# Modulation chunks in pairs over one bank, placed in norms and attention; scores ahead of older transposes; low parts on one engine

## The reference, cut to what matters

```python
# two hybrid layers (l = 0, 1), each:
shift, scale, gate = split(silu(c) @ w_mod[l] + b_mod[l], 3)          # 1024 -> 3 x 1024, also for c_ctx
h = rms_norm(x, norm_w) * (1 + scale) + shift
p = h @ w_in ;  y = [MLA attention 6 heads, GQA attention 6 heads, conv] * silu(gate columns of p)
x = x + gate * (y @ w_out)
# then a second block of two layers (i = 0, 1):
sh1, sc1, g1, sh2, sc2, g2 = split(silu(c_2) @ ada_w[i] + ada_b[i], 6) # 1024 -> 6 x 1024
x = x + g1 * mixer(rms_norm(x) * (1 + sc1) + sh1)   # i=0: differential attention, 8 heads; i=1: Fourier mixing
x = x + g2 * ffn(rms_norm(x) * (1 + sc2) + sh2)     # i=0: dense SwiGLU (1024 -> 3584); i=1: 8 experts, top 2
return rms_norm(x, final_g)
```

## Time and profile before

| | us |
|---|---|
| median of 3 runs (range) | 2388.37 (2382.81 to 2389.44) |
| the profiled execution | 2385.09 |
| its span | 2382.4 |
| TensorE busy | 2231.7 (94%) |
| VectorE busy | 1297.4 (54%) |
| ScalarE busy | 1116.2 (47%) |
| GpSimd busy | 901.4 (38%) |

### The profile page before, as it was taken

The page is one execution under the profiler, slowest core; times in us unless marked ns, Lnnn a source line. Parts: engine busy times, 40 slices in busy tenths (PEclk is TensorE's granted clock), DMA queues, the critical chain, the costliest instruction groups (busy, mean ns, idle before and its releaser), DMA issues.

```text
span 2382.4 us, 29666 instructions
## 1 busy us (share of the span) xinstructions
PE 2231.7 (94%) x11321; PEld 1678.8 (70%) x11321; DVE 1297.4 (54%) x1619; ACT 1116.2 (47%) x1227; POOL 901.4 (38%) x353
## 2 busy tenths in 40 slices
PE   6999999999979978899998999999999999999997
PEld 3454564684764436899987787878787787878786
DVE  3702451614330343555432777777776768777775
ACT  3011440224220043344321776767676767767674
POOL 1000000000000000000000897979797988979794
PEclk8989999999989988999998999999999999999998
DMA  9203571226822252445744798989898998989890
GB/s 315 71 21 106 212 277 53 98 88 245 295 82 71 70 177 71 142 168 178 186 142 177 280 374 291 373 291 372 305 361 312 349 355 314 370 295 375 290 364 18
DMA packets 258525, 532.13 MB, mean 223 GB/s; under 512 B 5963, under 2 KB 41442, under 8 KB 258317
## 3 DMA queue, kind: packets, MB, share of 16 engines
q1 hardware_dynamic: 255808, 527.06, 62.0%
q10 hardware_dynamic: 2252, 3.80, 0.5%
q0 software_dynamic: 384, 0.14, 0.0%
HBM read 529.93 MB, written 1.05 MB: 223 GB/s over the span
## 4 chain that ended last, share of the span: by engine, by line
PE 53%; POOL 31%; issue 11%; DVE 4%; ACT 0%; DMA 0%; POOLq 0%; DVEq 0%
PE bank L634 48%; POOL ring_r L620 17%; POOL scratch_r L620 13%; PE bank L674 2%; PE bank L703 1%; PE bank L731 1%; DVE scratch L1579 1%; PE bank L890 1%; DVE nmax L1671 1%; DVE H L1612 0%; DMA scratch<-in_conv_dw_w 0%; DVE scratch L1858 0%; POOL scratch L612 0%; DVE scratch L1857 0%; DVE scratch L1665 0%
## 5 line engine op out<-in xcount | busy, mean ns | idle before, releaser
L620 POOL TENSOR_TENSOR ring_r<-ring,H_r 128x384 fp32r<-128x384 f32 x128 | 339.5, 2661 | 1410.9 <-ACT H_r L1494 1410.3
L634 PE MATMUL bank<-H_r,scratch_r 128*128 128x512 f32 (+1 forms) x2016 | 543.1, 347 | 17.5 <-DVE scratch_r L2020 11.9
L634 PE MATMUL bank<-H,ring 128*128 128x256 f32 (+2 forms) x1408 | 453.2, 484 | 7.5 <-ACT H L1275 6.1
L634 PE MATMUL bank<-scratch_r 128*128 128x512 f32 (+1 forms) x1696 | 419.8, 361 | 1.8 <-issue 1.8
L634 PEld LDWEIGHTS bank<-H,ring 128*128 128x128 f32 (+1 forms) x1408 | 270.4, 193 | 183.7 <-issue 159.3
L634 PEld LDWEIGHTS bank<-H_r,scratch_r 128*128 128x128 f32 x2016 | 350.7, 190 | 63.9 <-issue 17.1
L634 PEld LDWEIGHTS bank<-scratch_r 128*128 128x128 f32 x1696 | 304.1, 189 | 51.2 <-issue 2.0
L1494 ACT ACTIVATE H_r<-ring 128x2048 fp32r<-128x2048 f32 x128 | 244.7, 1917 | 99.3 <-PE bank L634 99.2
L2003 DVE TENSOR_TENSOR ring_r<-ring,H_r 128x1664 fp32r<-128x1664 f32 x128 | 254.7, 2000 | 57.5 <-ACT H_r L1494 56.1
L634 PE MATMUL bank<-H_r,modrow_r 128*128 128x512 f32 x672 | 263.2, 392 | 0.0
L620 POOL TENSOR_TENSOR scratch_r<-scratch,H_r 128x384 fp32r<-128x384 f32 x96 | 258.2, 2697 | 0.0
(11 more groups left out here) (189 smaller groups left out, 2655.3 us busy)
## 6 DMA issues: line engine op xcount, KB each, us to landing
ring<-in_moe_w SPq DMA_DIRECT2D x96, 2048.0 KB, 7.9
scratch<-in_moe_w SPq DMA_DIRECT2D x72, 2048.0 KB, 8.1
ring<-in_ada_w SPq DMA_DIRECT2D x24, 2048.0 KB, 8.1
ring<-in_ff_w SPq DMA_DIRECT2D x14, 2048.0 KB, 8.0
ring<-in_w_mod SPq DMA_DIRECT2D x12, 2048.0 KB, 9.0
ring<-in_ff_w SPq DMA_DIRECT2D x8, 1792.0 KB, 8.6
ring<-in_w_in SPq DMA_DIRECT2D x6, 2048.0 KB, 7.8
ring<-in_attn_w_qkv SPq DMA_DIRECT2D x6, 2048.0 KB, 8.0
```

The lines of the kernel that those rows point to most:

```text
L620: nc.gpsimd.tensor_tensor(low_half(h)[:, own], raw_half(h)[:, own], HI_PARTS[h % HI_RING][:, own].bitcast(F32), ALU.subtract).then_inc(lo_ ...
L634: m = nc.tensor.matmul(out_, w, x_, start=first, stop=last)
```

## The change

1. A modulation unit is now one part of 1024 columns, that is two chunks, whose "mod first" matmuls (16) go into one bank: `mod_half(mp, 0)` writes rows 0 and 1 of each group of 32, `mod_half(mp, 1)` rows 2 and 3 (the condition columns are shifted by two in `cond`). One ScalarE copy, one "mod second" of four matmuls with four selector columns, and one VectorE add follow for the pair.
2. The places are new. At the start still four chunks. Attention of layer 0: 6 chunks; layer 1: 4; differential attention: 10. Norms 1 to 6 take one pair each: half 0 ahead of `norm_sums`, half 1 ahead of the spreading of the roots, "mod second" behind it. The order of the weight chunks follows.
3. `attention_steps` yields "scores" of unit s ahead of "transposes" of unit s-2.
4. In the experts' loop VectorE makes the whole low part (2048 columns), and GpSimd none.

```diff
+FIRST = [(0, 0), (0, 1)]
+FILL = [[(0, 2), (1, 0), (1, 1)], [(2, 0), (2, 1)], [(2, 4), (2, 5), (3, 0), (3, 1), (3, 2)]]
+NORM_FILL = {1: [(1, 2)], 2: [(2, 2)], 3: [(2, 3)], 4: [(3, 3)], 5: [(3, 4)], 6: [(3, 5)]}
...
-    return (mods(0)[:4] + inner0 + mods(0)[4:] + mods(1) + mods2[:MODS2_FIRST] + out0 + inner1 + mods2[MODS2_FIRST:]
-            + mods3[:MODS3_FIRST] + out1 + qkv + mods3[MODS3_FIRST:] + wo + ff + fo)
+    return (mods(FIRST) + inner0 + mods(FILL[0]) + out0 + mods(NORM_FILL[1]) + inner1 + mods(FILL[1]) + out1
+            + mods(NORM_FILL[2]) + mods(NORM_FILL[3]) + qkv + mods(FILL[2]) + wo + mods(NORM_FILL[4]) + ff
+            + mods(NORM_FILL[5]) + fo + mods(NORM_FILL[6]))
...
             for s in range(units + 3):
+                if s < units:
+                    yield "scores", s
                 if 2 <= s < units + 2:
                     yield "transposes", s - 2
                 if s < units:
-                    yield "scores", s
                     yield "exps", s
...
+            def mod_half(mp, half):
+                m, part = mp
+                if half == 0:
+                    row_turn[mp] = (t.g % 8, t.g // 8)
+                    start()
+                b = row_turn[mp][0]
+                s, w = chunk(f"mod{m}.{2 * part + half}")
                 for r in range(2):
                     for q in range(4):
-                        last = product(bank[b][32 * q:32 * q + 32, :], cond[:, m // 2, 2 * q + r, :],
-                                       w[:, 2 * q + r, :], r == 0, r == 1)
-                last.then_inc(bank_ready[b], 1)
+                        last = product(bank[b][32 * q:32 * q + 32, :],
+                                       cond[:, m // 2, 2 * q + r, 2 - 2 * half:34 - 2 * half],
+                                       w[:, 2 * q + r, :], half == 0 and r == 0, half == 1 and r == 1)
+                if half:
+                    last.then_inc(bank_ready[b], 1)
                 release.append(weights_used[s])
...
             def norm(i):
+                fill = NORM_FILL.get(i, [])
+                for mp in fill:
+                    mod_half(mp, 0)
                 if i:
                     norm_sums(i)
+                for mp in fill:
+                    mod_half(mp, 1)
                 spread_roots([(None, 0, 1, norm_params(i)[0])])
+                for mp in fill:
+                    mod_pair("mod second", mp)
...
-                        own = slice(0, DVE_SHARE)
-                        v.tensor_tensor(low_half(i)[:, own], raw_half(i)[:, own],
-                                        HI_PARTS[i % HI_RING][:, own].bitcast(F32), ALU.subtract).then_inc(lo_ready, 1)
+                        v.tensor_tensor(low_half(i), raw_half(i), HI_PARTS[i % HI_RING].bitcast(F32),
+                                        ALU.subtract).then_inc(lo_ready, 1)
```

More of the change, by code:

```diff
@@ L130, in constant_table @@
     t[:, T_UPPER:T_UPPER + P] = (i[:, None] < i[None, :])
-    t[:, T_SEL] = i % 32 == 0
-    t[:, T_SEL + 1] = i % 32 == 1
+    for j in range(4):
+        t[:, T_SEL + j] = i % 32 == j
     t[:, T_PART] = i
@@ L159, in cols, with mods @@
         return [(w[:, c0:c1].rearrange("(k p) n -> p k n", p=P), c1 - c0, 0)]
-    def mods(m):
-        w = (a["w_mod"][0], a["w_mod"][1], a["ada_w_2"][0], a["ada_w_2"][1])[m]
-        return [(f"mod{m}.{c}", cols(w, 512 * c, 512 * c + 512)) for c in range(w.shape[1] // 512)]
+    def mods(parts):
+        out = []
+        for m, part in parts:
+            w = (a["w_mod"][0], a["w_mod"][1], a["ada_w_2"][0], a["ada_w_2"][1])[m]
+            out += [(f"mod{m}.{c}", cols(w, 512 * c, 512 * c + 512)) for c in (2 * part, 2 * part + 1)]
+        return out
     def layer(l):
@@ L222, in build @@
         mod = [sb(f"mod{m}", [P, (24, 24, 48, 48)[m], 2]) for m in range(4)]
-        cond = sb("cond", [P, 2, KT, 32])
+        cond = sb("cond", [P, 2, KT, 34])
         root = sb("root", [P, 4, 48])
@@ L613, in _ @@
             nc.gpsimd.memset(UP_FLAT, 0.0).then_inc(pads_clear, 1)
-            pool.wait_ge(list_ready, 1)
-            passes = pool.value_load(LIST[0:1, 12:13], min_val=EXPERTS, max_val=EXPERTS + OVER)
-            with pool.Fori(0, passes) as j:
-                for h in range(HALVES):
-                    pool.wait_ge(hi_ready, j * HALVES + (SPLIT_BEFORE + h + 1))
-                    own = slice(DVE_SHARE, HALF)
-                    nc.gpsimd.tensor_tensor(low_half(h)[:, own], raw_half(h)[:, own],
-                                            HI_PARTS[h % HI_RING][:, own].bitcast(F32), ALU.subtract).then_inc(lo_rest_ready, 1)
         @block.tensor
@@ L702, in mod_pair @@
                     for j in range(4):
-                        last = nc.tensor.matmul(bank[b][:, 2 * j:2 * j + 2], modrow[:, c % 2, P * j:P * j + P],
-                                                tab[:, T_SEL:T_SEL + 2], start=True, stop=True)
+                        last = nc.tensor.matmul(bank[b][:, 4 * j:4 * j + 4], modrow[:, 0, P * j:P * j + P],
+                                                tab[:, T_SEL:T_SEL + 4], start=True, stop=True)
                     last.then_inc(bank_ready[b], 1)
@@ L929, in _ @@
             pe.wait_ge(cond_ready, 2)
-            for c in range(4):
-                mod_pair("mod first", (0, c))
-                if c:
-                    mod_pair("mod second", (0, c - 1))
-            mod_pair("mod second", (0, 3))
+            mod_pair("mod first", FIRST[0])
+            mod_half(FIRST[1], 0)
+            mod_pair("mod second", FIRST[0])
+            mod_half(FIRST[1], 1)
+            mod_pair("mod second", FIRST[1])
             for l in range(2):
@@ L1232, in mod_step @@
                 if what == "mod first":
-                    take(ACT.Copy, modrow[:, mc[1] % 2, :], bank[b][:, :], b, n)
+                    take(ACT.Copy, modrow[:, 0, :], bank[b][:, :], b, n)
             def seed(columns):
@@ L1257, in norm @@
                 n_tok, m, _, shift, _ = norm_params(i)
+                fill = NORM_FILL.get(i, [])
+                fill_turns = [t.next() for _ in fill]
                 if i:
@@ L1260, in norm @@
                 rb, rn = t.next()
+                for b, n in fill_turns:
+                    take(ACT.Copy, modrow[:, 0, :], bank[b][:, :], b, n)
+                    t.skip(1)
                 if m is None:
@@ L1380, in _ @@
             for s in range(2):
-                nc.scalar.activation(cond[:, s, :, 0:2], vec[:, :, R_C + 2 * s:R_C + 2 * s + 2],
+                nc.scalar.activation(cond[:, s, :, 2:4], vec[:, :, R_C + 2 * s:R_C + 2 * s + 2],
                                      ACT.Silu).then_inc(cond_ready, 1)
             norm_squares(0, x)
-            for c in range(4):
-                mod_step("mod first", (0, c))
-                if c:
-                    mod_step("mod second", (0, c - 1))
-            mod_step("mod second", (0, 3))
+            for what, mp in zip(("mod first", "mod first", "mod second", "mod second"), FIRST + FIRST):
+                mod_step(what, mp)
             for l in range(2):
@@ L1587, in norm @@
                 n_tok, m, scale, _, r = norm_params(i)
+                fill = NORM_FILL.get(i, [])
+                t.skip(len(fill))
                 if m is not None:
```

45 lines of the change are left out of this document (19 added, 26 removed).

## The result

The changed kernel takes 2315.52 us (median of 4 runs, 2315.10 to 2315.72) against 2386.15 for the kernel before on the same chip: a ratio of 0.970, 95% interval 0.969 to 0.972. The forecast was 2330, its range 2302 to 2362. The profiled execution took 2315.1 with a span of 2313.3, 69.1 less than before.

What follows compares the result with a forecast made beforehand. The chain of waits ran 53% over TensorE; GpSimd's 31% was called misleading. The terms summed to -56.7 us from the profiled 2385.1, or 2328.4; half of a 3.3 us median offset made it 2330, range 2302 to 2362.

Steps and rivals of the forecast that it cites:

- attention of layer 0: Layer 0's attention: 8 fewer "mod first" at 1.86 us and 11 fewer "mod second" at 0.98, 25.7 us less.
- attention of layer 1: Layer 1's attention: 8 fewer "mod first" at 1.86 us and 10 fewer "mod second" at 0.98, 24.7 us less.
- new waits there: Layers 0 and 1: 3 us allowed for new latency waits over 36 attention units, bounds 0 and 25.
- differential attention: Scores first breaks the serial loop of waits; steps without a pair 2.9 us, stage 72.5 against 91.5, 19 us less.
- start: Kernel start: two of four "mod second" go, the last follows its own ScalarE copy; 1 us less.
- norms 1, 2, 3, 5, 6: Modulation halves partly hidden in these norms' TensorE gaps; together 6.5 us more, bounds 3 and 12.
- norm 4: Norm 4: `w3.0` waits for `wo1`'s slot, delaying ScalarE's split and squares; 17.2 us more, bounds 12 and 21.
- experts: Experts' loop: waits at pass starts shrink without GpSimd, 1.6 us a pass, 13 us less; bounds 19 less and 0.
- fills hid waits: Rival: in layers 0 and 1 units without modulation run at their own chain, half of 50 us stays; 2355, chance 0.12.
- half clock: Rival: thinner attention units drop the clock; layers 0 and 1 at half clock give about 2450; chance 0.02.
- The slower rival: Experts: VectorE too slow for all low parts, deciding from 2.7 us each; 2498 at 3.2 us; chance 0.05.
- the clock gives back: Rival, joined with norm 4 not being late: denser TensorE work keeps the clock up; 2310, chance 0.13.

Runs made afterwards that it cites:

- scores_first_only: Kernel before with only the scores of unit s put ahead of the transposes of unit s-2: 2353.47 us, ratio 0.986.
- split_order: Changed kernel with the second and third feed-forward splits moved behind norm 4, on ScalarE and VectorE: 2298.73 us, ratio 0.963.
- pair_out: Changed kernel with norm 4's modulation pair moved to the end of the differential attention's fill, ScalarE's order kept: 2305.28 us, ratio 0.965.
- vector_low_only: Kernel before with only the experts' whole low part given to VectorE and none to GpSimd: 2371.40 us, ratio 0.993.
- gpsimd_beside: Changed kernel with GpSimd making one unused 128x384 subtraction of zeros per high part in the experts' loop: 2326.25 us, ratio 0.974.

## Why the prediction was right

| step | predicted | measured, from the two traces |
|---|---|---|
| attention of layer 0 | -25.7 | -24.7 |
| attention of layer 1 | -24.7 | -24.3 |
| new waits there | +3 | 0 |
| differential attention | -19 | -20.6 |
| start | -1 | -0.9 |
| norms 1, 2, 3, 5, 6 | +6.5 | +3.0 |
| norm 4 | +17.2 | +17.6 |
| experts | -13 | -15.1 |
| all else | 0 | -4.6 |
| sum | -56.7 | -69.6 to the end of the experts |

- **Layers 0 and 1.** Right to 1.4 us, by counting matmuls at their pitch. The 3 us for new waits did not come: TensorE is busy 86.40 of 86.40 and 55.49 of 55.50. Of the rivals, "fills hid waits" fell with it, and so did half clock there (0.96 and 0.95). The time that I gave the half-clock rival was miscounted: 2330 and 142 more are 2472, not 2450.
- **Differential attention.** The mechanism was right: the step is now VectorE's 2.78 us (I took 2.9), and without the order the stage takes 95.8 (my upper bound for a loop that stays was 98). The size was right in part by luck. Some 13 us of the gain come by the clock, 0.85 before and 0.98 now (`scores_first_only` shows as much), and I named that only as a rival. It is in my 72.5 all the same: the step that I priced, like the 1.86 and 0.98 of a pair, stands in rows at the upper clock, though the stage as a whole did not. I gave no reason why all steps should run like this one. Its window in the kernel before, with the granted clock at 1.00:

```profile
886.20:890.86 4.66, 2.80 (x16) 1.69 (x17) 2.75 (x6) 2.38 (x7) 0.00 (x0) 1.00 1.01 385
```

- **Norm 4.** Right in size and in each link: release by half 0, 7.7 us to landing, split, squares, sums 917.21 - 896.02 = 21.2 us after T (predicted 20.8), then half 1 at half clock (3.64). `split_order` and `pair_out` break the chain at two links and take back 16.6 and 17.6 us of norm 4's time.
- **The other norms.** Half of what I allowed. Norms 2 and 3 together cost 2.0, not 3.7, norm 1 nothing. The gap of norm 3 took up what norm 2 was late by, and though half 1 ran there at 3.24, the spreading behind it was back at 1.16, where it took 2.08 before. Behind norm 1 the clock stood higher than in the earlier trace rows, 0.83 instead of 0.74; in norm 4 (second row) it is 0.50 still:

```profile
398.00:408.00 10.00, 9.80 (x35) 7.27 (x36) 4.80 (x14) 7.04 (x16) 0.00 (x0) 0.83 0.62 210
914.70:924.70 10.00, 7.26 (x33) 4.21 (x33) 4.43 (x10) 1.77 (x4) 0.00 (x0) 0.50 0.34 116
```

- **Experts.** 1.9 us a pass, not 1.6, and not as I had it. The listed waits fell by 9.3 us in seven passes, 1.3 a pass; the other 0.6 is in TensorE's busy time, which fits the prediction's words that the products behind a wait also start late. `vector_low_only` gives 17.4 in all. The 15 that the prediction drew from the Trainium skill, "SBUF — State Buffer", section "Who interferes with whom", came nearer to that than my 13, but by luck: it took all waits for low parts as lock waits that would go, and those for VectorE's stayed (3.6 and 3.8). Nor does show that the longest instructions of the two engines met; it gives lengths alone. The slower rival decided at a mean low part of 2.7 us. In `gpsimd_beside` the 294 low parts of seven passes last 2.65 us in the mean (2.29 in the changed kernel); VectorE is busy 868 of 912 us, and 1.2 us a pass are already lost. No run went past the point, so where it lies is not shown; what is shown is that a loss begins before it.
- **All else.** -4.6 us in stages that the change does not touch: layer 0 ahead of its attention -2.6 (clock 0.94 before, 0.96 now), layer 1 ahead of its own +1.5 (0.94, 0.93), Fourier mixing -1.8 (0.96, 1.00), router -1.4, the rest small. Each of the first three goes the way of its clock, but each is also within what two single profiles can differ by (last section), so that the change caused them is not shown. By span x 2 x (1 - granted clock) TensorE stood for an estimated 176 us of the kernel before at the lower of its two clocks (1.2 and 2.4 GHz) and for 139 of the changed one; by the same working 27 and 3 of these are the differential attention's, most of the difference. I had the clock only in the rival "the clock gives back", at a chance of 0.13 and together with a norm 4 that is not late. Half of that rival came true: norm 4 was late, and the clock gave back. The 13 us by which the time fell short of the sum are these 4.6, 3.5 in the norms, 3 of waits that did not come, and about 2 or less in each of the others.

## What to carry to other kernels

When work is moved to where an engine idles, follow its loads through the ring: they push later loads to slots that come free later, and here one queue order, two instructions that waited for such a load ahead of others, gave 17 us back. Put filling work ahead of the gap, not behind it (5.7 us in two norms here, by the medians), and price it at the clock that holds there. When a stage stands below full clock, price its steps both ways and say which you take. A second engine that takes a share of elementwise work can cost more than its share when both read SBUF: measure the pass with the share at zero.
